# Head outputs copied to x unscaled, inverses turned four steps later, and the second mixer weighed two head pairs at a time

## The reference, cut to what matters

```python
# mixer A: 8 heads of 64, band of 9 chunks of 64 keys, bias by distance
p = jax.nn.softmax(sc, axis=-1)
out = jnp.einsum('bhqk,bkhd->bqhd', p.astype(vc.dtype), vc)
# mixer B: 8 query heads, 2 key heads, band of 2 chunks, a sink per head
m = jnp.maximum(jnp.max(sc, axis=-1, keepdims=True), sink)
p = jnp.exp(sc - m)
p = p / (jnp.sum(p, axis=-1, keepdims=True) + jnp.exp(sink - m))
o = jnp.einsum('bnhgqk,bnkhd->bnqhgd', p.astype(vb.dtype), vb)
```

## Time and profile before

| | us |
|---|---|
| median of 3 runs | 2696.72 |
| fastest and slowest of them | 2693.64, 2698.53 |
| the profiled execution, its own time | 2693.37 |
| its span, first to last instruction | 2691.3 |

### The profile page before, as it was taken

How to read it: one execution, slowest core, us unless ns; L and a number is a source line. 1 busy time by engine, 2 the same in 40 slices (tenths; PEclk the granted TensorE clock), 3 DMA queues, 4 the chain that set the end, 5 groups by cost and what they waited for, 6 DMA issues and landing times. The chain is left out here.

```text
span 2691.3 us, 36792 instructions
## 1 busy us (share of the span) xinstructions
PE 2620.4 (97%) x12920; PEld 2140.1 (80%) x12920; DVE 1922.8 (71%) x3579; ACT 1152.2 (43%) x2365; POOL 300.5 (11%) x518
## 2 busy tenths in 40 slices
PE   8999899999999999999999998999999999999998
PEld 6888777788888888888778886677888888888887
DVE  8766666654787787768996666666548887777687
ACT  6222577632533333344542226776325333333444
POOL 0000212244100000000000012223440000000000
PEclk9999999999999999999999999999999999999999
DMA  4333433253222332385423243332531322334843
GB/s 154 118 110 114 147 100 103 73 186 118 86 98 102 114 118 84 107 271 172 149 104 120 102 146 110 112 96 91 189 120 59 118 102 92 105 114 132 267 125 125
DMA packets 185397, 333.22 MB, mean 124 GB/s; under 512 B 17280, under 2 KB 62976, under 8 KB 185216
## 3 DMA queue, kind: packets, MB, share of 16 engines
q1 hardware_dynamic: 176992, 307.67, 34.6%
q10 hardware_dynamic: 8224, 23.20, 2.5%
HBM read 237.09 MB, written 92.80 MB: 123 GB/s over the span
## 5 line engine op out<-in xcount | busy, mean ns | idle before, releaser
L1278 PE MATMUL ps<-op_hi,up_hi 128*128 128x512 f32 x1232 | 479.9, 390 | 2.5 <-DVE third_sum L2870 2.5
L1280 PE MATMUL ps<-op_hi,up_lo 128*128 128x512 f32 x1232 | 479.4, 389 | 0.0
L1279 PE MATMUL ps<-op_lo,up_hi 128*128 128x512 f32 x1232 | 479.4, 389 | 0.0
L1278 PE MATMUL ps<-in_hi,up_hi 128*128 128x512 f32 x728 | 285.3, 392 | 2.1 <-DVE up_lo L2366 2.1
L1279 PE MATMUL ps<-in_lo,up_hi 128*128 128x512 f32 x728 | 283.9, 390 | 0.0
L1280 PE MATMUL ps<-in_hi,up_lo 128*128 128x512 f32 x728 | 283.9, 390 | 0.0
L1965 ACT ACTIVATE up_hi<-up_raw 128x512 fp32r<-128x512 f32 x252 | 158.1, 630 | 278.5 <-PE ps L1280 271.3
L1278 PEld LDWEIGHTS ps<-op_hi,up_hi 128*128 128x128 f32 x1232 | 231.3, 188 | 50.8 <-issue 3.3
L1280 PEld LDWEIGHTS ps<-op_hi,up_lo 128*128 128x128 f32 x1232 | 231.3, 188 | 48.1
L1279 PEld LDWEIGHTS ps<-op_lo,up_hi 128*128 128x128 f32 x1232 | 231.3, 188 | 47.9
L1278 PE MATMUL ps<-act_hi,dn_hi 128*128 128x512 f32 x616 | 240.5, 390 | 1.7 <-DVE dn_lo L3045 1.7
(11 more groups left out here) (266 smaller groups left out, 5265.4 us busy)
## 6 DMA issues: line engine op xcount, KB each, us to landing
up_raw<-w_gu SPq DMA_DIRECT2D x42, 1024.0 KB, 5.1
act_raw<-ff_saved SPq DMA_DIRECT2D x154, 256.0 KB, 2.8
w_quarter<-w_lin SPq DMA_DIRECT2D x52, 512.0 KB, 4.4
w_raw<-w_lin SPq DMA_DIRECT2D x48, 512.0 KB, 3.7
ff_saved<-ff_block SPq DMA_DIRECT2D x88, 256.0 KB, 2.0
ff_saved<-ff_mix SPq DMA_DIRECT2D x66, 256.0 KB, 2.1
gated<-gates_saved SPq DMA_DIRECT2D x32, 512.0 KB, 4.1
stage<-in_saved SPq DMA_DIRECT2D x48, 256.0 KB, 2.8
```

Of the source, the lines that this page charges most:

```text
L1278: pe.matmul(out, w1, x1, start=first, stop=False, skip_group_check=True)
L1279: pe.matmul(out, w1, x0, start=False, stop=False, skip_group_check=True)
L1280: return pe.matmul(out, w0, x1, start=False, stop=last, skip_group_check=True)
```

## The change

- take_wide on ACT becomes take_heads: ACT copies the weighed values, unscaled, from o_ps to x_sb, after head_done, and signals head_free.
- take_heads on DVE becomes scale_heads: DVE multiplies the turned inverses, read from w_ps, onto x_sb, after head_free and wide_turned, and signals head_scaled, which takes the place of wide_ready.
- turn_wide at step s is for the pair that ends with unit s-7 (before s-3), scale_heads for s-8 (before s-4), repeat_inverse on POOL for s-4 (before s-2). The loops run four steps longer.
- weigh keeps its step u+3 in mixer A and for the odd pairs of mixer B; for the even pairs of mixer B it goes to u+5. So p0 and p1 are weighed at one step, p2 and p3 four steps later, and so on.
- turn_wide and turn_values wait for head_scaled of the last inverse that was turned, that is, for DVE, where they waited for ACT.

```diff
+def weighed_at(u):
+
+    mixer, _, _, p = unit(u)
+    return u + (5 if mixer == "B" and p % 2 == 0 else 3)
+
+
+def weighed_in(s):
+    return [u for u in (s - 5, s - 3) if 0 < u < UNITS and u % 2 and weighed_at(u) == s]
...
-                    if s >= 3 and s % 2 == 1:
-                        repeat_inverse(L, s - 2)
+                    if s >= 5 and s % 2 == 1:
+                        repeat_inverse(L, s - 4)
...
                 if n > 0:
-                    pe.wait_ge(wide_ready, n)
+                    pe.wait_ge(head_scaled, n)
...
-                    if s >= 4 and s % 2 == 0:
-                        turn_wide(L, s, s - 3)
-                        weigh(L, s - 3)
+                    if s >= 8 and s % 2 == 0:
+                        turn_wide(L, s, s - 7)
+                    for u in weighed_in(s):
+                        weigh(L, u)
...
-                        if s > 3:
-                            pe.wait_ge(wide_ready, L * HEAD_PAIRS + (s - 2) // 2)
+                        if s >= 8:
+                            pe.wait_ge(head_scaled, L * HEAD_PAIRS + (s - 6) // 2)
                         turn_values(L, c, part)
...
-                act.wait_ge(wide_turned, L * HEAD_PAIRS + u // 2 + 1)
-                src = w_ps if mixer == "A" else w_ps.rearrange("p (h n) -> p h n", h=2)
-                act.activation(x_of(u), src, ACT.Copy).then_inc(wide_ready, 1)
+                act.wait_ge(head_done, L * HEAD_PAIRS + u // 2 + 1)
+                src = o_ps(u) if mixer == "A" else o_ps(u).rearrange("p (h n) -> p h n", h=2)
+                act.activation(x_of(u), src, ACT.Copy).then_inc(head_free, 1)
...
-                    if s >= 5 and s % 2 == 1:
-                        take_wide(L, s - 4)
+                    for u in weighed_in(s - 1):
+                        take_heads(L, u)
...
             def split_o(L):
-                act.wait_ge(head_free, (L + 1) * HEAD_PAIRS)
+                act.wait_ge(head_scaled, (L + 1) * HEAD_PAIRS)
...
-                dve.wait_ge(head_done, n + 1)
-                dve.wait_ge(wide_ready, n + 1)
-                src = o_ps(u) if mixer == "A" else o_ps(u).rearrange("p (h n) -> p h n", h=2)
-                dve.tensor_tensor(x_of(u), src, x_of(u), ALU.mult).then_inc(head_free, 1)
+                dve.wait_ge(head_free, n + 1)
+                dve.wait_ge(wide_turned, n + 1)
+                inverse = w_ps if mixer == "A" else w_ps.rearrange("p (h n) -> p h n", h=2)
+                dve.tensor_tensor(x_of(u), inverse, x_of(u), ALU.mult).then_inc(head_scaled, 1)
...
-                    if s % 2 == 1 and s >= 5:
-                        take_heads(L, s - 4)
+                    if s % 2 == 1 and s >= 9:
+                        scale_heads(L, s - 8)
```

More of the change, by code:

```diff
@@ L766, in build @@
         wide_turned = sem("wide_turned")
-        wide_ready = sem("wide_ready")
+        head_scaled = sem("head_scaled")
         sq_ready = sem("sq_ready")
@@ L1250, in _ @@
                 split(L, 1)
-                for s in range(UNITS + 2):
-                    if s >= 3 and s % 2 == 1:
-                        repeat_inverse(L, s - 2)
+                for s in range(UNITS + 4):
+                    if s >= 5 and s % 2 == 1:
+                        repeat_inverse(L, s - 4)
                     for t, part in split_parts(s):
@@ L1504, in attention @@
                 pe.wait_ge(in_taken, in_takes(L, IN_PAIRS - 1, 6))
-                for s in range(UNITS + 3):
+                for s in range(UNITS + 7):
                     if s < UNITS:
@@ L1845, in take_turned, with take_heads @@
                 act.activation(turned_to(u)[:, 0:cols], t_ps[:, 0:cols], ACT.Copy).then_inc(turned_ready, 1)
-            def take_wide(L, u):
+            def take_heads(L, u):
                 if u == 1:
@@ L2709, in invert_pair, with scale_heads @@
                 dve.reciprocal(st[:, :, 6:7], total).then_inc(inverse_ready, 1)
-            def take_heads(L, u):
+            def scale_heads(L, u):
                 mixer, _, _, _ = unit(u)
                 n = L * HEAD_PAIRS + u // 2
-                dve.wait_ge(head_done, n + 1)
-                dve.wait_ge(wide_ready, n + 1)
-                src = o_ps(u) if mixer == "A" else o_ps(u).rearrange("p (h n) -> p h n", h=2)
-                dve.tensor_tensor(x_of(u), src, x_of(u), ALU.mult).then_inc(head_free, 1)
+                dve.wait_ge(head_free, n + 1)
+                dve.wait_ge(wide_turned, n + 1)
+                inverse = w_ps if mixer == "A" else w_ps.rearrange("p (h n) -> p h n", h=2)
+                dve.tensor_tensor(x_of(u), inverse, x_of(u), ALU.mult).then_inc(head_scaled, 1)
             def scale_logit(L, i, b):
@@ L2733, in attention @@
             def attention(L):
-                for s in range(UNITS + 4):
+                for s in range(UNITS + 8):
                     if s < UNITS:
                         row_max(L, s)
-                    if s % 2 == 1 and s >= 5:
-                        take_heads(L, s - 4)
+                    if s % 2 == 1 and s >= 9:
+                        scale_heads(L, s - 8)
                     if s % 2 == 0 and 1 <= s <= UNITS:
```

## The result

| | median, us | runs | lowest, highest |
|---|---|---|---|
| before | 2696.72 | 13 | 2693.62, 2700.36 |
| changed | 2701.71 | 13 | 2698.04, 2705.29 |

The ratio is 1.0018, interval [1.0011, 1.0025]: 5.0 us slower. I had forecast 2695.5, no measurable change. The time lies inside the stated range, close to the slower rival's 2701.9, but the effect is real and has the other sign than the sum, so the forecast was wrong.

The account below looks back on a forecast made before the run. TensorE, busy 97% of the span, was taken as the bound, through its matmuls and waits in the attention. Gains and losses summed to +1.2 us, giving 2695.5 us against the 2696.72 median, range 2689.5 to 2703.

Parts of the forecast that it names:

- slower rival: Head of phase B: all of ACT's standing reaches PE, 1.42 us in each of 8 phases; 2701.9 us, chance 0.19.
- The end: Behind the last scores: three last turn_wides in series with DVE's product delay the gate 1.32 us a layer, -2.6.
- Group 0: First group's phase B, played through: new head wait, first two merges and value turns, +0.6; p4 with p5's merge, +0.7.
- Value turns keep the waits in front of turn_wide: Ahead of turn_wide in mid-attention: PE still waits for ACT's value turns, so the later inverse gains 0 there.
- The merges and the unfilled steps: Weighing two pairs in one run, 0.34 us each, +6.1 and +0.7; unfilled steps losing their weighing, +2.7.
- The wait at the head of phase B: p1's weighing waits for ACT's copy behind p0's weighing: 0.70 us each, -4.2 for groups 1 to 3.
- turn_wide and value turns behind DVE's product: At unfilled steps turn_wide waits for DVE's later product, -1.7; value turns wait for it at two steps, -0.8.
- a rival of its own: PE's clock in group 0: shifted phases drop a slow stretch or add one or two; 2694.2 to 2698, chance 0.06.
- The start of the attention: Steps 4 and 6: two turn_wides no longer run there, +0.4 for both layers.

Follow-up runs that it names:

- the exchange's alone: Changed kernel with only the exchange of roles between ACT and DVE, turn_wide, POOL and DVE at the old steps, no merged weighings: 2698.07, ratio 1.0005 to the kernel before.
- the busy: Changed kernel plus 10, 4 and 4 unread transposes of the identity ahead of the last three turn_wides: 2699.50, ratio 1.0009; with the head wait relaxed too, 2691.26.
- the other end: Changed kernel with the last two turn_wides between the following gate's matmuls and DVE's last logit behind the product: 2696.96, ratio 1.0002 to the kernel before.

## Why the prediction was wrong

Three terms failed. DVE's product was put at -2.5 in two terms, and putting it first gave back 5.9. The end was put at -2.6 and came to -7.9, of which -3.9 at full clock. Group 0 was put at +1.3 and came to -3.2, of which -0.7 at full clock. Common to them is that each new wait was priced on start times of the trace of before, with PE at full speed.

*Value turns keep the waits in front of turn_wide:* right in the main, 12.5 us of 16.4 stayed, and 18.7 where DVE's product comes early.

*The merges and the unfilled steps, +9.5:* right in size, 9.4 measured where they are free to act (7.4 to 11.6, drawing again from the runs).

*The wait at the head of phase B, 0.70 each:* right for groups 1 to 3, 0.76 measured. Its step in group 0 failed. I had played that phase through on the times of before, and got +0.6 with the first merges in it. With p4 and p5's merge in, +1.3, it came to -0.7 at full clock and to -3.2 as profiled. The wait is worth 1.15 a layer there at full clock and 1.5 and 1.9 as profiled. ACT's idle time ahead of p1's copy is 1.43 us in layer 0 at full clock and 2.48 in the changed kernel, whose clock fell in it. Why the phase lost 0.4 a layer at full clock, where I had a gain, stays open. Group 3 added 0.44 two steps later, which I had not looked for. In all 6.3 us (8.2 with PE kept busy at the end) for 5.6.

*turn_wide and value turns behind DVE's product, -1.7 and -0.8:* failed in size at one clock, more than any other term. Putting the product first gave 5.9 (which may hold some time that the product took before the change as well). I had taken DVE's times from the trace of before and subtracted. But the product is placed behind the row maxima of its own step, and these follow scores that PE itself starts late after the waits above; in the changed trace a value turn at 462.88 waits 0.55 for it. DVE's times move with PE's, so I take a subtraction on old times to be too low as a rule; that is argued from this one wait. I had also read row 8's 1.41 of POOL as one operation, and it is two. What I left out of the sum for POOL's splits no run tests.

*The end, -2.6:* mechanism right, size wrong. At full clock it is 8.64 against 6.67, 2.0 a layer (forecast 1.3). DVE's logit starts 3.04 behind the last scores, not 2.68, and eight weighing matmuls stand between two of the turn_wides. Then the clock: I had made it a rival of its own, tied to group 0, with 0.06. It belongs to this term, and to group 0's: there I had 1.3 us for a fall, the price of a piece, where the whole phase lost 0.4 by it before and 1.3 to 1.6 with the change. At the end PE idles 1.43 and 0.50 us between small operations, and the gates behind start at 1.2 GHz in three of the four ends of the changed kernel that were profiled, and in none of before's, of the exchange's alone, of the busy or of the other end. The Trainium skill ("TensorE: Matmul & The Clock Gate", section "What's actually happening") says that an idle PE drops to 1.2 GHz. The trace agrees in the level, 0.63 us for a matmul of 0.39, though PE was not quite idle before it: it was busy for 3.30 us of 525:530.

*The start of the attention, +0.4:* a gain that I missed. Before, PE waited 1.17 us for ka_lo, since DVE stood in front of it for the product of the first pair, which needs weighing and ACT's copy. DVE, before:

```profile
298.86 0.29 DVE L2718 TENSOR_TENSOR x_sb<-ps,x_sb 128x128 f32<-128x128 f32 x1 [1.09 <-ACT x_sb L1856]
299.06 0.68 DVE L2638 TENSOR_TENSOR ka_lo<-stage,ka_hi 128x512 fp32r<-128x512 f32 x1
```

With the product four steps later ka_lo comes first: 1.55 a layer, +3.1. It is the lag's doing, as the kernels with only the exchange (no gain) and without merges (all of it) show.

*The slower rival* named the right place and nearly the right time, 2701.9, by the wrong sum, so that was luck: the head of phase B did not cost 1.42 in all eight phases but 0.76 in groups 1 and 2, 1.2 in group 3 and 1.15 to 1.9 in group 0, and the rest of the loss was at the end and on DVE, less a gain at the start.

What is not settled: how much of the 1.5 us between 3.5 (at one mean clock) and 5.0 is the end's clock and how much other falls of the clock. Group 0's comes and goes in nearly every kernel here, and so do those outside the attention, near 42 and 1370 us.

## What to carry to other kernels

When an operation is moved later in a loop, look at both ends: what it no longer stands in front of at the start, and how many serial round trips it leaves behind the last iteration, where nothing fills them and PE's clock can fall as well. A wait that cost nothing because its condition was always two steps old must be read again when that condition is moved; here one count that was stricter than its buffer needs cost 6 us. When a new dependency goes to another engine, ask where in that engine's own step the releasing operation stands: putting it first was worth 6 us, and no engine had less to do.

## What the hardware showed

Doing more on PE made the kernel faster: 18 transposes a layer into a bank that nothing reads took 2.3 us off one kernel and 4.3 off another, by keeping the granted clock at 1.00 behind the attention. The same instructions, with starts that agreed for 14 us, went on at full clock in one execution and at half speed in another, which cost 1.3 us in a phase of 31. And the spread of a kernel's runs goes with the mean granted clock, 2692.8 us at 0.998 and 2699.5 at 0.994 for the kernel before, so that a sum made against one profiled execution should first ask at which clock it ran.
